# Two jobs of a projection split their k tiles 4 and 12 instead of 8 and 8

## What is computed

```python
mod = c @ w_ada + b_ada                       # six vectors of 2048: sh1, sc1, gt1, sh2, sc2, gt2
h = modulate(rmsnorm(x, g_mix), sh1, sc1)     # h * (1 + sc1) + sh1
proj = h @ w_in                               # columns: qa 1024, ka 128, va 128, qr, kr, vr, gr 1024 each
y = concat(attention(qa, ka, va), silu(gr) * group_norm(retention(qr, kr, vr))) @ w_out
x = x + gt1 * y
x = x + gt2 * (relu(modulate(rmsnorm(x, g_ffn), sh2, sc2) @ w1) ** 2 @ w2)
out = rmsnorm(x, g_final)
```

## Time and profile before

| | us |
|---|---|
| median of 3 runs (lowest, highest) | 1176.98 (1175.03, 1178.56) |
| span of the profiled execution | 1176.1 |
| TensorE busy | 1132.5 (96%) |
| VectorE busy | 795.4 (68%) |
| ScalarE busy | 492.5 (42%) |

### The profile page before, as it was taken

The page is one execution under the profiler, slowest core; times in us unless marked ns, Lnnn a source line. Parts: engine busy times, 40 slices in busy tenths (PEclk is TensorE's granted clock), DMA queues, the critical chain, the costliest instruction groups (busy, mean ns, idle before and its releaser), DMA issues.

```text
span 1176.1 us, 15924 instructions
## 1 busy us (share of the span) xinstructions
PE 1132.5 (96%) x6339; PEld 957.8 (81%) x6339; DVE 795.4 (68%) x690; ACT 492.5 (42%) x517; POOL 21.1 (2%) x27
## 2 busy tenths in 40 slices
PE   3879999999999999999999999999999999999996
PEld 1769989788778878888888888888888888888885
DVE  2577889987878898866565566565566565565675
ACT  2424454555534445443333444333444333444451
POOL 2000010000000001000000000000000000000000
PEclk9999999999999998999999999999999999999999
DMA  9999989999997956766666676666676666665551
GB/s 351 368 348 397 381 319 339 338 403 390 357 404 269 322 182 223 252 222 229 235 230 185 188 222 228 235 228 186 187 220 229 238 224 187 187 196 180 180 177 72
DMA packets 156749, 303.10 MB, mean 258 GB/s; under 512 B 5425, under 2 KB 73633, under 8 KB 148129
## 3 DMA queue, kind: packets, MB, share of 16 engines
q1 hardware_dynamic: 155248, 298.08, 72.4%
q10 hardware_dynamic: 832, 2.93, 0.6%
q0 software_dynamic: 624, 1.48, 0.4%
HBM read 300.36 MB, written 2.10 MB: 257 GB/s over the span
## 4 chain that ended last, share of the span: by engine, by line
PE 91%; DVE 4%; DMA 3%; issue 1%; ACT 1%; ACTq 0%; SPq 0%; DVEq 0%
PE ps_job L924 20%; PE ps_job L963 14%; PE ps_job L964 14%; PE ps_job L965 14%; PE ps_job L927 10%; PE ps_job L939 3%; PE ps_job L940 3%; PE ps_job L941 3%; DMA stage<-in_w_ada 2%; PE ps L1030 1%; DVE acc L1247 1%; DVE w_lo L1323 1%; DMA cst<-in_consts 1%; PE ps_job L1211 1%; PE ps_job L1209 1%
## 5 line engine op out<-in xcount | busy, mean ns | idle before, releaser
L1323 DVE TENSOR_TENSOR w_lo<-stage,w_hi 128x2048 fp32r<-128x2048 f32 x164 | 375.8, 2292 | 218.5 <-ACT w_hi L518 218.3
L518 ACT ACTIVATE w_hi<-stage 128x2048 fp32r<-128x2048 f32 (+1 forms) x167 | 318.0, 1904 | 424.0 <-PE ps_job L965 231.4
L924 PE MATMUL ps_job<-act_hl,w_hi 128*128 128x512 f32 x1024 | 322.4, 396 | 1.5 <-DVE w_lo L1323 1.1
L927 PEld LDWEIGHTS ps_job<-act_hl,w_lo 128*128 128x128 f32 x1024 | 192.7, 188 | 45.0
L927 PE MATMUL ps_job<-act_hl,w_lo 128*128 128x256 f32 x1024 | 201.2, 278 | 0.0
L963 PE MATMUL ps_job<-w_hi,hid_hl 128*128 128x512 f32 x480 | 188.1, 392 | 0.0
L964 PE MATMUL ps_job<-w_lo,hid_hl 128*128 128x512 f32 x480 | 187.0, 390 | 0.0
L965 PE MATMUL ps_job<-w_hi,hid_hl 128*128 128x512 f32 x480 | 186.9, 389 | 0.0
L924 PEld LDWEIGHTS ps_job<-act_hl,w_hi 128*128 128x128 f32 x1024 | 156.1, 189 | 2.5 <-DVE w_lo L1323 1.3
L1247 DVE SCALAR_TENSOR_TENSOR acc<-stage,small,acc 128x2048 f32<-128x2048 f32 (+1 forms) x56 | 122.9, 2195 | 7.2 <-DMA stage<-in_w_ada 3.5
L963 PEld LDWEIGHTS ps_job<-w_hi,hid_hl 128*128 128x128 f32 x480 | 90.1, 188 | 19.2 <-issue 0.7
(11 more groups left out here) (223 smaller groups left out, 1127.1 us busy)
## 6 DMA issues: line engine op xcount, KB each, us to landing
stage<-in_w SPq DMA_DIRECT2D x128, 1024.0 KB, 5.3
stage<-in_w_ada SPq DMA_DIRECT2D x64, 1024.0 KB, 7.8
stage<-in_w_in SPq DMA_DIRECT2D x41, 1024.0 KB, 8.5
stage<-in_w_ada SPq DMA_DIRECT2D x32, 512.0 KB, 6.9
stage<-in_w_out SPq DMA_DIRECT2D x16, 1024.0 KB, 7.7
gate_rows<-in_w_ada SPq DMA_DIRECT2D x16, 1024.0 KB, 7.0
x_sb<-in_x ACTq DMA_DIRECT2D x1, 2048.0 KB, 13.5
out_y<-f_acc SPq DMA_DIRECT2D x3, 512.0 KB, 2.7
```

The lines of the kernel that those rows point to most:

```text
L518: nc.scalar.activation(w_hi[:, ring, 0:width], stage[:, slot, 0:width], ACT.Copy).then_inc(hi_ready, 1)
L924: nc.tensor.matmul(ps_job[:, 2 * pair + e, :], w_hi[:, ring, ws], act_hl[:, kt, :], start=(kt == 0), stop=False)
L927: last = nc.tensor.matmul(ps_job[:, 2 * pair + e, T:2 * T], w_lo[:, ring, ws], act_hl[:, kt, 0:T], start=False, stop=(kt == KT - 1))
L1323: nc.vector.tensor_tensor(w_lo[:, ring, 0:width], stage[:, slot, 0:width], w_hi[:, ring, 0:width].bitcast(F32), ALU.subtract).then_inc(lo_ ...
```

## The change

The two wide jobs of columns 1792 and 2304 (`EARLY`, half of qr and half of kr) had k tiles 0 to 7 before G_B and 8 to 15 after it. Now they have 0 to 3 in one group, and 4 to 15 in three groups after G_B. The first set so has six groups (`FIRST_SET`, `G_SET` = 6), and between the first set and G_B there are twelve groups where there were sixteen; G_B is group 18 where it was 20. The number of groups, loads, matmuls and row tiles is the same. The six groups' places: key and value columns, the two early jobs, then the three others. The PSUM banks of the two early jobs are used again by the second and third of these others, so the results of the early jobs leave PSUM inside the set.

The loads from the first group to the second group of the next set, in order (t is a row tile, g a group):

| | order of loads, from load 16 |
|---|---|
| before | g0, t16, t17, g1, t18 to t21, g2, t22 to t24, g3, t25 to t31, g4, t32, g5 |
| after | g0, t16, g1, t17 to t19, g2, t20 to t22, g3, t23 to t26, g4, t27 to t31, g5, g6, t32, g7 |

Before, t16 is summed ahead of g0, t18 and t20 behind g0, t22 and t24 behind g1, t26 to t30 behind g2. After, t16 is summed behind g0, t18 behind g1, t20 and t22 behind g2, t24 and t26 behind g3, t28 and t30 behind g4. The sixteen row tiles of the third set stand between g4 and G_B's neighbour g19 before (about one for each group), between g6 and g17 after (one and two by turns).

```diff
-def w_in_jobs(k0, between):
-    jobs = [("feat", KV0, k0, HALF)]
-    jobs += [("wide", Q0 + TOK_COLS * n, k0, HALF) for n in range(2)] + between
-    jobs += [("wide", QR0 + TOK_COLS * n, k0, HALF) for n in range(4)]
+SET_K = 4
+EARLY = (1, 2)
+def w_in_jobs(second):
+    k0 = HALF if second else 0
+    early = [("wide", QR0 + TOK_COLS * n, 0, SET_K) for n in EARLY]
+    jobs = [] if second else early
+    jobs += [("feat", KV0, k0, HALF)] + [("wide", Q0 + TOK_COLS * n, k0, HALF) for n in range(2)]
+    if second:
+        jobs += [("tok", VR0 + TOK_COLS, 0, KT)]
+        jobs += [("wide", QR0 + TOK_COLS * n, SET_K, KT - SET_K) if n in EARLY else ("wide", QR0 + TOK_COLS * n, k0, HALF) for n in range(4)]
+    else:
+        jobs += [("wide", QR0 + TOK_COLS * n, k0, HALF) for n in range(4) if n not in EARLY]
...
-GROUPS = [(j, q) for q in range(2) for j in range(OPEN)] + [(j, q) for j in range(OPEN, len(JOBS)) for q in range(N_GROUPS[j])]
+FIRST_SET = [(j, 0) for j in [J_KV, *range(J_KV), *range(J_KV + 1, J_CLOSED)]]
+GROUPS = FIRST_SET + [(j, 1) for j in range(J_KV, J_CLOSED)] + [(j, q) for j in range(J_CLOSED, len(JOBS)) for q in range(N_GROUPS[j])]
+G_SET = len(FIRST_SET)
...
-    second = min(KT, (0, 2, 6, 9)[g] if g < OPEN else KT)
+    second = (0, 1, 4, 7, 11, KT)[g] if g < G_SET else KT
...
-    return KT + second + min(KT, max(0, 16 * (g - OPEN) // 15)) + later
+    return KT + second + min(KT, max(0, 16 * (g - G_SET) // (G_B - 1 - G_SET))) + later
...
-            if j in (1, 2):
-                return [0, 1] if j == 1 else [4, 5]
-            if j in (0, OPEN - 1):
-                return [2] if j == 0 else [6, 7]
+            if j < J_CLOSED:
+                return [[0, 1], [4, 5], [2], [0, 1], [4, 5], [6, 7]][j]
...
-            sum_second(1)
...
-                if g + 2 <= OPEN:
-                    sum_second(g + 2)
+                if g < G_SET - 1:
+                    sum_second(g + 1)
```

More of the change, by code:

```diff
@@ L46 @@
 HALF = KT // 2
-def w_in_jobs(k0, between):
-    jobs = [("feat", KV0, k0, HALF)]
-    jobs += [("wide", Q0 + TOK_COLS * n, k0, HALF) for n in range(2)] + between
-    jobs += [("wide", QR0 + TOK_COLS * n, k0, HALF) for n in range(4)]
+SET_K = 4
[10 more added lines that the diff above has]
+        jobs += [("wide", QR0 + TOK_COLS * n, k0, HALF) for n in range(4) if n not in EARLY]
     jobs += [("tok", GR0 + TOK_COLS * n, k0, HALF) for n in range(2)]
     return jobs + [("tok", VR0, k0, HALF)]
-JOBS = w_in_jobs(0, []) + w_in_jobs(HALF, [("tok", VR0 + TOK_COLS, 0, KT)])
+JOBS = w_in_jobs(False) + w_in_jobs(True)
 JOBS += [("out_attn", TOK_COLS * n, 0, HALF) for n in range(STRIPS)]
 JOBS += [("out_ret", TOK_COLS * n, HALF, HALF) for n in range(STRIPS)]
-J_B = len(w_in_jobs(0, []))
+J_B = len(w_in_jobs(False))
 J_BQ, J_BGR = J_B + 1, J_B + 8
@@ L66 @@
 J_MLP = J_OR + STRIPS
-OPEN = 4
-N_GROUPS = [2] + [nk // (8 if kind == "feat" else 4) for kind, _, _, nk in JOBS[1:]]
-GROUPS = [(j, q) for q in range(2) for j in range(OPEN)] + [(j, q) for j in range(OPEN, len(JOBS)) for q in range(N_GROUPS[j])]
+J_KV = len(EARLY)
+J_CLOSED = J_KV + 4
+N_GROUPS = [2 if j == J_KV else nk // (8 if kind == "feat" else 4) for j, (kind, _, _, nk) in enumerate(JOBS)]
+FIRST_SET = [(j, 0) for j in [J_KV, *range(J_KV), *range(J_KV + 1, J_CLOSED)]]
+GROUPS = FIRST_SET + [(j, 1) for j in range(J_KV, J_CLOSED)] + [(j, q) for j in range(J_CLOSED, len(JOBS)) for q in range(N_GROUPS[j])]
+G_SET = len(FIRST_SET)
 FIRST = [GROUPS.index((j, 0)) for j in range(len(JOBS))]
@@ L88 @@
 CHUNKS_BEFORE = [0, 2, 4, 8]
-OPENING = [0, OPEN, G_B]
+OPENING = [0, G_SET, G_B]
 HEAD_COLS = 2 * FEAT_COLS
@@ L669, in _ @@
                     nc.scalar.activation(result_of(J_V), psum_of(J_V), ACT.Copy).then_inc(evacuated, 1)
-                if g == OPEN:
+                if g == G_SET:
                     modulate_segment(1)
@@ L1091, in _ @@
                     pe.wait_ge(ret_ready, 4 * q + 4)
-                if g in (2, 3):
-                    pe.wait_ge(turned_out, 2 * g + 2)
+                if g == 2:
+                    pe.wait_ge(turned_out, 6)
+                if g == G_SET - 1:
+                    pe.wait_ge(turned_out, 8)
                 if kind == "feat":
@@ L1096, in _ @@
                 elif kind == "wide":
-                    wide_group(k0 + 4 * q, (g - G_MLP) % 2, banks(j)[0], q == 0, q == N_GROUPS[j] - 1, g == OPEN - 1)
+                    wide_group(k0 + 4 * q, (g - G_MLP) % 2, banks(j)[0], q == 0, q == N_GROUPS[j] - 1, g == G_SET - 1)
                 else:
```

## The result

The changed kernel takes 1187.97 us (1186.05 to 1188.39) where the kernel before takes 1177.77: a ratio of 1.0086 (in brackets, here and below, its 95% interval: [1.0068, 1.0104]), some 10 us slower. The forecast was 1180.0, with a range up to 1185.0. The profiled execution has a span of 1186.0 us, 9.9 us longer than before, and its time is 1.8 us above its span.

A forecast was written before the change was run, and what follows sets the result against it. TensorE was taken as the bound (busy 96%), its opening holes waiting on the load stream. First set +0.6, with the second stage +3.2, after G_B 0; forecast +3.0 on 1176.98, 1180.0 us, range 1173.5 to 1185.0.

The forecast's parts named there:

- Steps 1 to 3: First set: group 1 at 43.7 us, no half clock; holes of 1.35 us before group 3, 3.35 before group 4.
- Step 4: Group 5 up to the second set's opening: a hole of 2.4 us, opening at 87.2 us, balance +0.6 us.
- steps 2 and 3: Groups 3 and 4: loads on a dry queue, 3.6 us per 0.5 MB, leave holes of 1.35 and 3.35 us.
- steps 2 to 4: Groups 3 to 5: ring slots freed late, then load, rounding and split, leave holes of 1.35, 3.35 and 2.4 us.
- Step 5: Second stage loses cover: the stream sets it, VectorE close behind; G_B at 161.1 us, sum so far +3.2 us.
- (c): Load stream up to group 17 falls to 356 GB/s; G_B at 168.3, sum +10.4, 1187 us; chance 0.03.
- Step 6: From G_B to the end: cost 0, bounds -1 to +1 us, no hole from 180 to 400 us.
- (a): Opening holes close, stream never runs dry: G_B at 153.2 to 155.5, gain 2.4 to 4.7, about 1173.4 us; chance 0.15.
- (b): Second stage: VectorE, waiting for ScalarE's rounding, makes it slower; G_B at 165, sum +7, 1184 us; chance 0.20.
- (d): Nothing moves: the third set is not late, only the first set's +0.6 us remains, 1177.6 us; chance 0.12.

## Why the prediction was wrong

**Steps 1 to 3 were right.** Group 1 starts at 43.63 (43.7 forecast), with no half clock near 45 (a mean of 1.00 from 40 to 50 us). Group 3 has a hole of 1.60 us (1.35) and group 4 one of 3.51 (3.35), and starts at 70.17 (69.55). The mechanism was the one I gave, slots that TensorE frees only behind a group, and its price held up to here.

**Step 4 failed, by two of its terms.** It had the second set open at 87.2; it opens at 92.65, 5.4 us later, of which 2.8 are the landing of group 5 and 2.7 its clock.

The landing: I had group 5 landed at 74.7 and usable at 79.0. ScalarE's timeline has its rounding at 77.52, as soon as it has landed, and TensorE starts it at 81.81, 2.8 us late. The roundings of groups 4 and 5 (with group 6), in the kernel after:

```profile
65.88 1.91 ACT L529 ACTIVATE w_hi<-stage 128x2048 fp32r<-128x2048 f32 x1 [7.71 <-DMA stage<-in_w_in]
...
77.52 2.86 ACT L529 ACTIVATE w_hi<-stage 128x2048 fp32r<-128x2048 f32 x2 [8.82 <-DMA stage<-in_w_in]
```

SP's issues of tiles 28, 29 and 31:

```profile
61.01 0.37 SPq L361 DMA_DIRECT2D stage<-in_w_ada  x1
...
66.29 0.37 SPq L361 DMA_DIRECT2D stage<-in_w_ada  x1
...
67.22 1.21 SPq L361 DMA_DIRECT2D stage<-in_w_ada  x1
```

size and time to landing of tile 28, of tile 31, and of group 5, which is issued between 70 and 71 us:

```profile
stage<-in_w_ada SPq DMA_DIRECT2D x1, 512.0 KB, 8.4
...
stage<-in_w_ada SPq DMA_DIRECT2D x1, 512.0 KB, 6.3
...
stage<-in_w_in SPq DMA_DIRECT2D x1, 1024.0 KB, 7.4
```

and the stream from the landing of group 4 to that of group 5:

```profile
66.00:77.50 11.50, 7.99 (x62) 7.43 (x52) 6.14 (x4) 2.70 (x2) 0.00 (x0) 0.85 0.94 319
```

I had tiles 27 to 31 and group 5 land behind group 4 at 388 GB/s, from 65.25 to 74.7, 9.45 us. Group 4 lands at 65.9, 0.6 us late, and the six loads, five of 0.52 MB and one of 1.05, then take 11.6 us, at some 315 GB/s: 2.2 of the 2.8 us are the rate, 0.6 the start. Two of the six are slow. Tile 28 lands at 69.4, 2.2 us after tile 27; SP queued nothing behind it until 66.29, when TensorE's sums behind group 3 (at 65.59) let the next slots go. And group 5 lands 4.0 us after tile 31, which lands at 73.5 (72.0 forecast). I had rows of a thin stream at hand and used them in steps 2 and 3, where the queue was dry, but not here, where it had just been. Why these loads don't get the full rate, the runs don't settle: with the sooner sums the same six take 10.9 us (337 GB/s) between the roundings of groups 4 and 5, and with the twelfth gap they were slower still, 11.9. The two roundings in the kernel with the sooner sums:

```profile
61.59 1.92 ACT L529 ACTIVATE w_hi<-stage 128x2048 fp32r<-128x2048 f32 x1 [5.27 <-DMA stage<-in_w_in]
...
72.49 1.91 ACT L529 ACTIVATE w_hi<-stage 128x2048 fp32r<-128x2048 f32 x1 [8.08 <-DMA stage<-in_w_in]
```

The clock: I took no half clock and gave "0 or 1.7 us" as its bounds. Stretches of one microsecond of the kernel after, within group 5:

```profile
83.00:84.00 1.00, 1.00 (x7) 1.00 (x6) 0.00 (x0) 0.00 (x0) 0.00 (x0) 0.50 0.94 317
...
86.00:87.00 1.00, 1.00 (x7) 1.00 (x5) 0.00 (x0) 0.00 (x0) 0.00 (x0) 0.50 1.05 412
```

The stretch from 80 to 90 us has a mean of 0.66, so 0.34 x 10 / 0.5 = 6.8 us at the lower level, of which some 5.5 fall on group 5, from 81.81 to about 87.3; at half speed that is 2.7 us lost. The forecast's own sentence said that a slow group 5 would not be hidden, and it named a half clock that falls elsewhere as a sign of being wrong. Its price was from rows of 3.4 us at the lower level; here the level lasted twice as long. The run with filled holes confirms the size: 2.4 us sooner. How long it lasts is in part chance. The three kernels with halves left out have the same first set, with holes of 2.49, 3.05 and 2.24 us ahead of group 5; their mean clock from 80 to 90 us is 0.83, 1.00 and 0.83, and their second sets open at 93.03, 90.40 and 91.81. The stretch in the one with half of the loads, behind its hole of 3.05 us:

```profile
80.00:90.00 10.00, 7.20 (x60) 6.46 (x60) 4.43 (x8) 1.63 (x4) 0.00 (x0) 1.00 0.94 361
```

The late sums stand behind both terms. With the sooner sums group 5 starts at 76.79 instead of 81.81, 5.0 us sooner: 4.3 because the loads behind group 4 start sooner, 0.7 because they run faster. Of the 2.7 us of the lower clock 1.7 are left. The forecast named the late slots, in steps 2 to 4, but priced them with a stream that is at its full rate as soon as the slots are there.

**Step 5 was right,** in size (2.5 us lost, 2.6 forecast) and in kind: the stream sets the stage, VectorE close behind. Its holes lie where it said, the largest 1.64 us at 146.83, released by a split; the three runs with halves left out show that the two limits are nearly equal. The 1.7 us of lower clock that I had repeat in this stage did not come (a mean of 1.00 from 92.65 to 166.46 us), which hardly matters where TensorE waits for weights. The stream's rate of 401 GB/s in that stage also ends rival (c), which had it fall to 356. The Trainium skill (DMA: Bandwidth & Descriptors, Specifications) gives about 358 GB/s as a core's share of HBM; with this one core at work the trace does not agree, by 401 over 20 us.

**Step 6 missed 1.3 us,** just outside its bounds of -1 to +1. TensorE has a hole of 1.90 at 180.30, released by `tmp` on VectorE, which is late from a row sum of the next vector. VectorE's row for that sum, after and then before:

```profile
175.09 2.35 DVE L1259 SCALAR_TENSOR_TENSOR acc<-stage,small,acc 128x2048 f32<-128x2048 f32 x1 [2.84 <-DMA acc<-in_b_ada]
```

```profile
176.10 2.35 DVE L1247 SCALAR_TENSOR_TENSOR acc<-stage,small,acc 128x2048 f32<-128x2048 f32 x1 [0.95 <-DMA acc<-in_b_ada]
```

It waits for a bias row of 8 KB that GpSimd's queue loads. After and then before, its size and time to landing:

```profile
acc<-in_b_ada POOLq DMA_DIRECT2D x1, 8.0 KB, 3.7
```

```profile
acc<-in_b_ada POOLq DMA_DIRECT2D x1, 8.0 KB, 1.8
```

That this small load is slower because more large ones are in flight is my reading of it, not shown by a run. In the runs with the sooner sums, with the tiles spread, and with both there is no loss behind G_B, and the load took 2.4, 2.6 and 2.0 us; in the one with the split taken ahead it took 3.1, and there is again a loss of 0.9.

**The rivals.** (a) fell: even with the sooner sums G_B comes at 161.5, with the tiles spread as well at 158.9, and not at 153 to 155. (c) came nearest in time, 1187, by a fall of the rate that did not come; (b), 1184, is from the wrong place too: VectorE alone does not set the stage. (d) fell with the first set. The chance of 0.43 for slower came from (b), (c) and the upper part of the forecast's own range; the range ended too low because step 4 had no bound for a rate between dry and full, and too small a one for the lower clock.

What stays open: why the five row tiles and group 5 move at 284 to 337 GB/s, and how fast one job alone would be with a better spread of its tiles.

## What to carry to other kernels

When work is moved ahead in a pipeline with a ring of buffers, list for every buffer who frees it and behind what that instruction is queued on its engine; here moving the sums by one group was worth 7 of the 10 us. Work that covers loads is not moved from one place to another for nothing: here the stage that it left had two nearly equal limits (stream and VectorE) and lost 2.5 us, and lowering one of two equal limits shows little, so test them singly and together. A hole ahead of a long group is priced with the slower clock that may follow it, and loads on a queue that has just been dry with the rate of such a stretch, not that of the full stream.

## What the runs showed of the hardware

- The stream's rate is not given by its being busy: over five loads of 512 KB and one of 1 MB it moved 319 GB/s at a share of 0.94 of the engines; in another kernel 284 at 0.92 over the tiles, then 424 at 1.05 with two loads of 1 MB.
- The lower clock doesn't follow from a hole's length alone. After the holes of 3.51 and 3.15 us the clock was at 0.50 for about 3.4 and 6.8 us; after one of 3.05 us at the same place in another kernel it stayed at 1.00; a hole of 2.71 us before was followed by it, one of 2.70 us at 98.67 after was not, a hole of 1.94 us was followed by it with the sooner sums (a mean of 0.91 from 130 to 150 us), one of 1.64 us in the same stretch of the kernel after was not (1.00).
- An 8 KB load on GpSimd's queue took 3.7 us in the kernel after and 1.8 before.
